# Opening of a two-layer decoder trunk: memory tile 0 loaded in two column halves, one weight load moved behind it

## The reference

```python
mk, mv = jnp.split(mem @ w_mem_kv[i], 2, axis=-1)
h = x @ a_w_in[j]
q, k, v, qm = jnp.split(h, [DIL_WIDTH, 2 * DIL_WIDTH, 3 * DIL_WIDTH], axis=-1)
...
def memory_attention(qm, mk, mv):
    s = jnp.einsum('bshd,bmhd->bhsm', qm, mk).astype(jnp.float32) * (HEAD_DIM ** -0.5)
    p = jax.nn.softmax(s, axis=-1).astype(mv.dtype)
    return jnp.einsum('bhsm,bmhd->bshd', p, mv)
```

## Time and profile before

| what | value |
| --- | --- |
| time, median of 3 runs | 2280.38 us (2278.51 to 2280.42) |
| the profiled execution's own time | 2277.74 us |
| its span, first to last instruction | 2276.0 us |
| mean granted TensorE clock | 0.997 |
| PE busy | 2229.9 us (98%) |
| DVE, ACT, POOL busy | 1241.8, 864.1, 1130.1 us |
| DMA | 128.23 MB, 56 GB/s over the span |

### The profile page before, as it was taken

The page is one execution under the profiler, slowest core; times in us unless marked ns, Lnnn a source line. Parts: engine busy times, 40 slices in busy tenths (PEclk is TensorE's granted clock), DMA queues, the critical chain, the costliest instruction groups (busy, mean ns, idle before and its releaser), DMA issues.

```text
span 2276.0 us, 32371 instructions
## 1 busy us (share of the span) xinstructions
PE 2229.9 (98%) x11304; PEld 1889.3 (83%) x11304; DVE 1241.8 (55%) x2361; ACT 864.1 (38%) x1622; POOL 1130.1 (50%) x681
## 2 busy tenths in 40 slices
PE   8999999999999999999999999999999999999997
PEld 7888888788888888888888889988888888888886
DVE  5555556657545454545555646667535444445446
ACT  5656666613432232332214743204332223232313
POOL 4221122563765555555553593442865555555543
PEclk9999999999999999999999999999999999999998
DMA  4111111141011111111131221221011111111121
GB/s 168 56 47 38 40 46 40 35 148 38 19 56 55 55 55 55 51 43 49 51 102 39 64 61 43 75 56 37 1 56 55 55 55 55 55 55 55 38 73 74
DMA packets 161548, 128.23 MB, mean 56 GB/s; under 512 B 11568, under 2 KB 147376, under 8 KB 161456
## 3 DMA queue, kind: packets, MB, share of 16 engines
q1 hardware_dynamic: 148992, 115.36, 16.6%
q10 hardware_dynamic: 12464, 11.63, 1.7%
HBM read 122.78 MB, written 4.19 MB: 56 GB/s over the span
## 4 chain that ended last, share of the span: by engine, by line
PE 91%; DVE 5%; ACT 2%; issue 1%; DMA 1%; POOL 0%; SPq 0%; DVEq 0%; ACTq 0%
PE ps L292 27%; PE ps L294 27%; PE ps L293 27%; PE ps L639 2%; PE ps L667 1%; PE ps L626 1%; PE ps L668 1%; PE ps L627 1%; PE ps L1419 1%; PE ps L1041 1%; DVE XR L1011 1%; DVE st L1098 1%; DMA raw<-in_a_w_in 1%; DVE V L1949 0%; PE ps L958 0%
## 5 line engine op out<-in xcount | busy, mean ns | idle before, releaser
L1696 DVE TENSOR_TENSOR XR<-XR,ps 128x512 f32<-128x512 f32 x576 | 378.7, 684 | 184.6 <-PE ps L294 184.6
L282 POOL TENSOR_TENSOR Wh<-raw,zcol 128x1024 fp32r<-128x1024 f32 x79 | 150.7, 1907 | 508.9 <-PE ps L294 412.2
L1619 POOL TENSOR_TENSOR Rl<-raw,Rh 128x512 fp32r<-128x512 f32 x216 | 279.2, 1293 | 198.8 <-ACT Rh L1550 198.8
L292 PE MATMUL ps<-Wdh,hidh 128*128 128x512 f32 x640 | 249.2, 389 | 1.3 <-DVE XR L1696 1.3
L292 PE MATMUL ps<-XTh,Wh 128*128 128x512 f32 x608 | 248.7, 409 | 1.3 <-DVE XTl L974 0.7
L293 PE MATMUL ps<-Wdl,hidh 128*128 128x512 f32 x640 | 249.0, 389 | 0.0
L294 PE MATMUL ps<-Wdh,hidl 128*128 128x512 f32 x640 | 249.0, 389 | 0.0
L294 PE MATMUL ps<-XTh,Wl 128*128 128x512 f32 x608 | 238.1, 392 | 0.0
L293 PE MATMUL ps<-XTl,Wh 128*128 128x512 f32 x608 | 237.7, 391 | 0.0
L1550 ACT ACTIVATE Rh<-raw 128x512 fp32r<-128x512 f32 x216 | 135.3, 626 | 257.3 <-PE ps L294 253.5
L292 PE MATMUL ps<-XTh,Rh 128*128 128x512 f32 x576 | 224.1, 389 | 0.0
(11 more groups left out here) (231 smaller groups left out, 4937.6 us busy)
## 6 DMA issues: line engine op xcount, KB each, us to landing
raw<-in_w_gate SPq DMA_DIRECT2D x44, 512.0 KB, 4.6
raw<-in_w_up SPq DMA_DIRECT2D x44, 512.0 KB, 3.9
rawd<-in_w_down SPq DMA_DIRECT2D x36, 512.0 KB, 3.5
raw<-in_a_w_in SPq DMA_DIRECT2D x20, 512.0 KB, 3.7
raw<-in_w_out SPq DMA_DIRECT2D x16, 512.0 KB, 3.5
raw<-in_b_w_in SPq DMA_DIRECT2D x15, 512.0 KB, 3.8
B<-in_c_bias SPq DMA_DIRECT2D x12, 512.0 KB, 3.5
raw<-in_w_mem_kv SPq DMA_DIRECT2D x8, 512.0 KB, 3.8
```

What stands on the lines that cost most here:

```text
L282: nc.gpsimd.tensor_tensor(high, raw[:, turn, :], zcol[:, 0:1].to_broadcast([P, UNIT]), ALU.add).then_inc(high_done, 1)
L292: nc.tensor.matmul(dst, wh, xh, start=first, stop=False, skip_group_check=onto)
L1619: nc.gpsimd.tensor_tensor(Rl[(w - 1) % 4][:, :], source(w), Rh[(w - 1) % 4][:, :].bitcast(F32), ALU.subtract).then_inc(gs[L]("low"), 1)
L1696: nc.vector.tensor_tensor(x, x, bank(4 + n % 4), ALU.add).then_inc(gf[L]("added"), 1)
```

## The change

Memory tile 0 is loaded by two transfers of 512 columns each (256 KB, `mem_half0` and `mem_half1`) in place of one of 1024 columns; tile 1 is loaded as before under the name `mem_tile1`. PE starts to turn tile 0 when half 0 has landed, and waits for half 1 ahead of its fifth transpose, by a new argument `middle` of `turn_pe`. SP waits for half 1 before it issues load 1 (p = 0, j = 1), the queries' weights of pair 0.

```diff
-    def turn_pe(pe, g, t, src, nk=KT, bb=0, after=None):
+    def turn_pe(pe, g, t, src, nk=KT, bb=0, after=None, middle=None):
 
         if t >= 2:
             pe.wait_ge(*g("xt_low", t - 1 if after is None else after))
         b = bb + 2 * (t % 2)
         for k in range(nk):
+            if k == 4 and middle:
+                middle()
             mm = nc.tensor.transpose(bank(b + k // 4, P, (k % 4) * P), src(k), ident[:, :])
         mm.then_inc(g("xt_turned"), 1)
...
                 for j in range(3):
+                    if (p, j) == (0, 1):
+                        sp.wait_ge(sem("mem_half1"), 16)
                     load(sp, 3 * p + j, src[letters(p)[j]])
...
-        for t in range(2):
-            pe.wait_ge(sem(f"mem_tile{t}"), 16)
-            turn_pe(pe, gm[0], t, columns(memraw[:, t, :]), bb=4)
+        pe.wait_ge(sem("mem_half0"), 16)
+        turn_pe(pe, gm[0], 0, columns(memraw[:, 0, :]), bb=4, middle=lambda: pe.wait_ge(sem("mem_half1"), 16))
+        pe.wait_ge(sem("mem_tile1"), 16)
+        turn_pe(pe, gm[0], 1, columns(memraw[:, 1, :]), bb=4)
         turn_x(0)
...
-        for t in range(2):
-            act.dma_start(memraw[:, t, :], mem[:, t, :]).then_inc(sem(f"mem_tile{t}"), 16)
+        for h in range(2):
+            act.dma_start(memraw[:, 0, h * 512:(h + 1) * 512], mem[:, 0, h * 512:(h + 1) * 512]
+                          ).then_inc(sem(f"mem_half{h}"), 16)
+        act.dma_start(memraw[:, 1, :], mem[:, 1, :]).then_inc(sem("mem_tile1"), 16)
```

## The result

The changed kernel takes 2283.8 us (median of 20 runs, 2282.01 to 2285.68) against 2278.76 us (20 runs, 2276.54 to 2280.57). The ratio is 1.0022, 95% interval 1.0016 to 1.0028: 5.0 us slower, just over the 0.2% that can be told from no change. The profiled execution took 2285.28 us for a span of 2283.6 us, so it lies 1.5 us above the median.

What follows compares the result with a forecast made beforehand. PE, busy 98% of the span, bounds the kernel, and the queries' weights pace its opening. Late weights (+3.2 us) and a lower clock (+1.4 us) add 4.6 us to 2280.38, giving 2285.0 us, range 2281.6 to 2286.9 us.

Steps and rivals of the forecast that it cites:

- SP's wait is the term that matters: Opening: load 1, issued near 6.85 us, lands at 20.2 us, 3.2 us later; queries start at 24.75 us, +3.2 us.
- The 0.7 us that PE waits for XTl: Start of the queries: read as a wait containing 0.3 us for Wl, so the x path is some 0.3 us earlier.
- The count of packets: SP's queue: load 1's 1024 packets flow from about 7.95 us at 84 a microsecond, 12.2 us, until 20.1 us.
- The working by bytes: DMA engines: x tiles land at about 20.2 us instead of 20.9, with only a few packets of load 1 left behind.
- The round robin: DMA engines alternate packet by packet between queues with work, so load 1 has an even share with x at once.
- The third case: Load 1 gets 182 packets a microsecond for its first 1.75 us, lands at 18.2 us; +1.2 us, 2281.6 us; chance 0.12.
- The clock: Opening: PE stands 4.2 us, the granted clock falls to 0.50 for some 3.4 us; +1.4 us, bounds 0 and 3.2.
- my fifth case: Clock low for two stretches, or load 1 a microsecond later still: +6 us or more, 2286.4 us and up; chance 0.05.
- The halves and PE's wait in the middle: Memory tile 0: extra issue and wait cost nothing; PE's path through memory tiles, keys and x some 0.65 us earlier.
- Nothing behind takes the loss back: After the opening: the next wait of note, 0.72 us at 34.34 us, follows from the queries' own results.
- The sum: Whole kernel: +3.2 us for late weights and +1.4 us for the clock, +4.6 us, giving 2285.0 us.
- The rival that was not slower: Start of the queries: weights no limit, up to 0.65 us gained, 2279.7 us; needs landing by 17.0 us; chance 0.06.

Runs made afterwards that it cites:

- wait_only: Kernel before plus SP's wait for the whole memory tile 0 ahead of load 1, without the halves; ratio to before 1.0018 (1.0009 to 1.0027).
- halves_only: Changed kernel without SP's wait ahead of load 1, the two halves kept; ratio to before 0.9999 (0.9990 to 1.0008).
- x_behind: Changed kernel with x tiles 2 to 7 sent on SP's queue behind load 1 instead of ACT's; ratio to before 0.9991, in the repeat 0.9995.
- before_again: Kernel before, unchanged, executed once for its profile, no ratio; load 1 lands at 16.86 us, second half of the queries starts at 34.20 us.
- busy_again: Repeat of the changed kernel with 16 extra PE matmuls while it waits for the queries' weights; ratio to before 1.0010 (1.0001 to 1.0019).
- x_behind_whole: Kernel before, tile 0 whole and no SP wait, with x tiles 2 to 7 on SP's queue behind load 1; ratio to before 1.0018 (1.0009 to 1.0027).
- wait_ident: Changed kernel, but SP waits for the identity matrix instead of half 1 ahead of load 1; one execution, no ratio; load 1 lands at 20.16 us.
- wait_tile1: Changed kernel, but SP waits for memory tile 1 instead of half 1 ahead of load 1; one execution, no ratio; load 1 lands at 20.25 us.
- after_busy: Changed kernel with 16 extra PE matmuls while it waits for the queries' weights; ratio to before 1.0016 (1.0007 to 1.0025).
- halves_again: Repeat of the two halves without SP's wait, one execution, no ratio; load 1 lands at 11.3 us, second half of the queries at 36.04 us.

## Why the prediction was right, point by point

- **SP's wait is the term that matters; the landing of load 1 sets the queries.** Right. I forecast a landing at 20.2 us, queries at 24.75 us, +3.2 us; measured 20.44 us, 24.97 us, +3.4 us. `wait_only` has it from this edit alone, `halves_only` lacks it. Two readings on the way there were wrong and did no harm. The 0.7 us that PE waits for XTl belong to the second half of the queries at 34.34 us and are not a wait around the 0.3 us for Wl at 21.54 us; that the other path is 0.3 us earlier follows from the end of tile 5's turning, 21.20 us. And 950 of about 1024 packets are 93%, not 95%.
- **How the landing comes about.** The count of packets came out right by luck, from two errors that met. I let the packets of load 1 flow 1.1 us after the issue, as with idle engines; they came 3.6 us after it. Against that, I let them flow at 84 a microsecond to the end; the queue had 943 through by 19 us and went faster from 18 us on, since x was nearly through. The working by bytes held: x's last transfer was to land at about 20.2 us with only a few packets of load 1 behind it, and it landed at 20.02 us. The round robin of the Trainium skill, "DMA: Bandwidth & Descriptors", section "Queues, rings and completion order", agrees with this trace from 11 us on (84 packets of SP's queue beside 87 of ACT's in a microsecond), and I was right to go by it for load 1. Whether it also holds from 5 to 7 us in `halves_only`, 775 packets beside 146, isn't shown: the first of load 1's 16 arrivals is at 6.84 us there (8.95 us before), so a part of it was through long before the rest, and no view tells whether both queues had work on every engine then.
- **The third case (a fast start for load 1)** did not come: no packet before 10 us.
- **The clock.** That it falls was right, in all five profiles in which the landing was at 19.8 us or later and PE was left idle. The term was mis-sized: I took +1.4 us, and it measured 2.0 to 2.7 us, because the low stretch lasts 6.8 us each time and not 3.4 us as in the one row I had the earlier trace rows. The long stretch of my fifth case, with a chance of 0.05, is what happened in every such profile; its price of +6 us or more is near what the marks give (5.7 and 6.2 us) and above what the medians give (5.0 us).
- **The halves and PE's wait in the middle cost nothing.** Right for the changed kernel, where PE's path is 0.97 us earlier (I took 0.65 us). I gave the halves no risk of their own; without SP's wait the marks show one, 1.1 to 1.7 us at the second half of the queries, though the time of `halves_only` (ratio 0.9999) shows no loss.
- **Nothing behind takes the loss back.** Right. From the second half of the queries to the end the profile of before has 2276.0 - 34.34 = 2241.7 us, that of after 2283.6 - 40.52 = 2243.1 us, the repeat of after 2280.7 - 40.01 = 2240.7 us. The spread goes with the clock's low stretches, below.
- **The sum.** +4.6 us forecast, 5.0 us measured (3.6 to 6.4 by the interval). In absolute terms I said 2285.0 us and 2283.8 us was measured; the kernel before was 1.6 us faster in this comparison than in the three runs that I started from. My chances leaned to no change (0.61, against 0.37 for slower), because +4.6 us lay right at the bound; the measured 5.0 us lies just beyond it, with an interval that reaches to both sides of the bound. By the marks it is 3.4 to 3.6 us of late weights and 2.0 to 2.7 us of clock, 5.7 to 6.2 us in two profiles, within the upper part of that interval. The rival that was not slower would have needed a landing by 17.0 us; it was nowhere near.

## What to carry to other kernels

A transfer held back so that another may land sooner doesn't lose only the time of the wait: it loses its place ahead of everything that is queued meanwhile, here 4 MB of x, and lands when those are nearly through, whether it was asked for at 3.7 or at 8.2 us. So hold it back only together with all that must not overtake it (the same queue, behind it, did this), and look first at which of two nearly equal paths the wait is put on. And price an idle stretch of PE twice: the stretch itself, and the matmuls behind it at the lower clock, 2.0 to 2.7 us behind a stand of 4.3 to 4.8 us.

## What the runs showed of the hardware

- A load issued while ACT's queue held the 4 MB of x had its first packets 3.6 to 3.8 us after the issue, whether that was at 3.66, 6.71 or 8.19 us. With 1 MB of x in ACT's queue and the engines nearly as busy it was 1.9 to 2.0 us (`x_behind` and its repeat), and with the engines idle about 1.1 us.
- Nearly the same number of packets of ACT's queue in two microseconds carried half the bytes, 0.27 MB for 0.54 MB: 128 of 2 KB and 2 of 4 KB in `halves_only`, 132 of 4 KB before, with 16 of 4 bytes each. SP's stream of 512 B filled the rest. A tile cut in two by columns has runs of half the length, and here that went with half the bytes beside another queue.
- The granted clock is down a second time near 1290 to 1304 us, where PE waits for DVE in layer 1, and for how long differs from run to run of the same kernel: not at all in one profile of the changed kernel, 6.8 us in the other. In three profiles (`before_again`, `busy_again`, `x_behind_whole`) it is also down for 3.4 us between 73.9 and 82.5 us. The rest of the span behind the second half of the queries follows the sum of these stretches: 2240.5 to 2240.7 us without any (the repeats of after and of `x_behind`, `wait_only`, `wait_ident`, `halves_only`), 2241.7 to 2242.1 us with 3.4 us (before, `x_behind`), 2243.0 to 2243.5 us with 6.8 us (after, `wait_tile1`, `after_busy`, `halves_again`) and 2244.6 to 2244.8 us with 10.2 us (the three named). That is 4.3 us of spread behind the part that was changed, nearly the effect measured here, and the reason to read marks in the trace beside the times.
- PE's transposes alone raised the clock: in the kernel before they took 424 ns in the mean until 11 us and 272 ns from 11.9 us on, and PE had done nothing else until 13.72 us. The clock's first record in that trace, at the full level, is at 11.60 us; ahead of it the clock's column reads 1.00 because it has no record. The moment differs between profiles, from 9.3 us (`busy_again`) to 16.2 us (`halves_again`), and 21.0 us in `x_behind_whole`. The Trainium skill, "TensorE: Matmul & The Clock Gate", section "Part 4: PE-mode transpose", says that transposes don't bring the engine to its full clock; here the trace disagrees.
